# A router's chain reordered: last normalized rows, code numbers and gates behind the choice's signal, first expert's rows ahead of the block numbers

## The reference

```
g_logits = xt @ w_group + b_group                 # 4 per token; xt: RMS-normalized rows
g_p, g_idx = top_k(softmax(g_logits), 1)
e_logits = (xt @ w_expert + b_expert)[.., 4, 8]   # the 8 of the chosen group
e_top, e_idx = top_k(e_logits[g_idx], 2)
gate = g_p * softmax(e_top)                       # two gates per token
for each expert e, over the tokens that chose it, in blocks:
    y = (silu(x @ w_gate[e]) * (x @ w_up[e])) @ w_down[e]
out[token] += gate * y
```

## Time and profile before

| | us |
|---|---|
| median of three runs | 1797.62 |
| profiled execution | 1796.66 |
| its span, first to last instruction | 1795.0 |
| TensorE matmuls busy | 1679.6 (94%) |
| VectorE busy | 654.4 (36%) |
| ScalarE busy | 381.2 (21%) |
| GpSimd busy | 219.4 (12%) |
| share of TensorE in the chain that ended last | 78% |
| share of DMAs in it | 9% |

### The profile page before, as it was taken

How to read it: one execution, slowest core, us unless ns; L and a number is a source line. 1 busy time by engine, 2 the same in 40 slices (tenths; PEclk the granted TensorE clock), 3 DMA queues, 4 the chain that set the end, 5 groups by cost and what they waited for, 6 DMA issues and landing times.

```text
span 1795.0 us, 27891 instructions
## 1 busy us (share of the span) xinstructions
PE 1679.6 (94%) x9786; PEld 828.0 (46%) x9787; DVE 654.4 (36%) x1597; ACT 381.2 (21%) x878; POOL 219.4 (12%) x313
## 2 busy tenths in 40 slices
PE   7899889989899999999997999999999999999984
PEld 5466665545444444444432444555434343444331
DVE  2334488832322222222211656764222222222113
ACT  2233355521111111111110234341111111111012
POOL 1232024400000101010101200000001010101000
PEclk9899999999899999999999999999899999999988
DMA  6153149784489999999997700226599999999974
GB/s 186 50 157 112 27 152 304 253 316 179 158 350 416 420 415 422 412 422 412 420 412 296 279 1 1 77 114 245 205 422 414 421 419 418 411 419 409 418 329 155
DMA packets 84883, 513.81 MB, mean 286 GB/s; under 512 B 20821, under 2 KB 43302, under 8 KB 58586
## 3 DMA queue, kind: packets, MB, share of 16 engines
q1 hardware_dynamic: 66378, 463.45, 64.0%
q0 software_dynamic: 18416, 49.16, 8.3%
HBM read 499.65 MB, written 26.52 MB: 293 GB/s over the span
## 4 chain that ended last, share of the span: by engine, by line
PE 78%; DMA 9%; DVE 6%; issue 2%; ACT 2%; DVEq 1%; SPq 1%; ACTq 1%; POOLq 0%
PE ps L2083 70%; PE ps L2088 8%; DMA mem<-in_moe_w_down 4%; DMA mem<-in_moe_w_up 2%; DMA mem<-in_cache_mla 2%; DVE mem L1366 1%; ACT mem L801 1%; SPq L482 1%; DVE mem L1861 0%; ACTq L978 0%; DMA mem<-in_mla_w_a 0%; DMA mem<-moe_rows_back 0%; DVE mem L1832 0%; DMA mem<-in_mla_wq_b 0%; DVE mem L1824 0%
## 5 line engine op out<-in xcount | busy, mean ns | idle before, releaser
L2083 PE MATMUL ps<-mem 128*64 128x512 f32 (+14 forms) x8402 | 1515.7, 478 | 70.5 <-DMA mem<-in_moe_w_down 15.1
L2083 PEld LDWEIGHTS ps<-mem 128*64 128x64 f32 (+5 forms) x8402 | 665.0, 147 | 834.9 <-issue 755.1
L801 ACT ACTIVATE mem<-ps 128x512 f32<-128x512 f32 (+7 forms) x358 | 193.5, 546 | 574.7 <-PE ps L2083 402.5
L2088 PE MATMUL ps<-mem 64*128 64x64 f32 (+3 forms) x1384 | 202.2, 281 | 37.4 <-ACTq L978 7.0
L2088 PEld LDWEIGHTS ps<-mem 64*128 64x128 f32 (+3 forms) x1384 | 168.1, 182 | 123.4 <-issue 96.0
L1700 DVE TENSOR_TENSOR mem<-mem,ps 64x512 f32<-64x512 f32 x64 | 44.1, 690 | 414.6 <-ACT mem L1044 414.5
L736 POOL DMA_INDIRECT moe_rows_back<-mem x64 | 57.3, 896 | 840.5 <-DVE mem L1718 818.9
L1044 ACT ACTIVATE mem<-ps 64x512 f32<-64x512 f32 x64 | 37.7, 589 | 535.5 <-PE ps L2083 535.5
L1718 DVE COPY mem<-ps 64x512 f32<-64x512 f32 x64 | 44.4, 693 | 162.0 <-PE ps L2083 162.0
L1366 DVE STREAM_TRANSPOSE mem<-mem 128x2560 f32<-128x2560 f32 x32 | 89.2, 2824 | 15.7 <-DMA mem<-in_cache_mla 15.5
L686 POOL DMA_DIRECT2D mem<-in_cache_mla x96 | 51.7, 538 | 75.2 <-PE ps L2083 68.1
(11 more groups left out here) (240 smaller groups left out, 517.5 us busy)
## 6 DMA issues: line engine op xcount, KB each, us to landing
mem<-in_moe_w_gate SPq DMA_DIRECT2D x64, 2048.0 KB
mem<-in_moe_w_up SPq DMA_DIRECT2D x64, 2048.0 KB
mem<-in_moe_w_down SPq DMA_DIRECT2D x64, 2048.0 KB
mem<-in_cache_mla POOLq DMA_DIRECT2D x160, 160.0 KB, 3.7
mem<-in_cache_mla SPq DMA_DIRECT2D x96, 160.0 KB, 4.5
mem<-moe_rows_back SPq DMA_DIRECT2D x8, 1024.0 KB, 9.0
mem<-in_mla_wkv_b SPq DMA_DIRECT2D x8, 512.0 KB, 5.7
mem<-in_mla_wo SPq DMA_DIRECT2D x1, 4096.0 KB, 14.2
```

Source lines behind the costliest of these rows:

```text
L801: return act.activation(out, in_, ACT.Copy)
L2083: return pe.matmul(out, lhsT, rhs, start=start, stop=stop)
L2088: return pe.transpose(out, in_, ident[at:at + n, at:at + n])
```

## The change

On ScalarE the last tile is squared before its transposed copy, and the root comes after it (`root_of`). On VectorE the last `normed` leaves its place ahead of the last `logits`; `experts` calls it after the marks of block 1. The signal `sel_ready` follows the masked marks at once; the difference for the second gate and the code numbers come after it, and two memsets go. The gates move from ahead of `rank_mm` to behind the last `normed`. Then come the copy of the first rows and, one at a time between the steps of block 0, the row numbers of blocks 0 and 1, the marks of block 2 with the operand of block 2's rows, and the count of blocks. TensorE makes the first rows ahead of both `numbers`, and issues eight warming matmuls instead of nine. All of it holds for both layers.

```diff
 
                 square(L, T)
                 act.drain()
+                root_of(L, T)
+
+            def root_of(L, T):
+
                 act.activation(rstd[:, T:T + 1], sumsq[:, T:T + 1], ACT.Sqrt, bias=eps[:, 0:1], scale=1.0 / D
                                ).then_inc(sig["root_ready"], 1)
 
...
                     square_and_root(L, 2)
                     turned(L, 1)
                     square_and_root(L, PT)
-                for n_ in range(2, TILES):
+                for n_ in range(2, PT):
                     turned(L, n_)
-                square_and_root(L, PT - 1)
+                square(L, PT - 1)
+                turned(L, PT)
+                act.drain()
+                root_of(L, PT - 1)
 
                 act.wait_ge(sig["gsub_ready"], happened("gsub_ready", L + 1))
                 act.activation(tg[1], tg[0], ACT.Exp).then_inc(sig["gexp_ready"], 1)
...
             logits(0, 3)
             turned(0, 4)
             inverse(0, PT - 1)
-            normed(0, PT - 1)
             logits(0, 4)
             v.drain()
 
...
                 v.scalar_tensor_tensor(out=te[0], in0=te[1], scalar=-3e30, in1=te[0], op0=ALU.mult, op1=ALU.add)
                 v.drain()
                 first_largest(te[0], NE, t5[6], t5[1], te[3], te[2])
+                v.tensor_tensor(te[3], te[1], te[2], ALU.add)
+                v.drain()
+                v.tensor_tensor(te[4], te[3], over_last(valid, NE), ALU.mult)
+                v.drain().then_inc(sig["sel_ready"], 1)
+
                 v.tensor_tensor(t5[4], t5[6], t5[3], ALU.subtract).then_inc(sig["esub_ready"], 1)
-
-                v.tensor_tensor(te[3], te[1], te[2], ALU.add)
-                v.memset(rankm, -1.0)
-                v.memset(code, 0.0)
-                v.drain()
-                v.tensor_tensor(te[4], te[3], over_last(valid, NE), ALU.mult)
                 v.tensor_copy(code[:, 0, :, 0:NE], over_last(tokcode[:, 0], NE))
                 v.tensor_tensor(code[:, 1, :, 0:NE], te[2], over_last(tokcode[:, 1], NE), ALU.add)
-                v.drain().then_inc(sig["sel_ready"], 1)
-
-                v.wait_ge(sig["gexp_ready"], happened("gexp_ready", L + 1))
-                v.tensor_reduce(t5[2], tg[1], X, ALU.add)
-                v.wait_ge(sig["eexp_ready"], happened("eexp_ready", L + 1))
-                v.tensor_scalar(t5[7], t5[5], 1.0, None, ALU.add)
-                v.drain()
-                v.tensor_tensor(t5[6], t5[2], t5[7], ALU.mult)
-                v.drain()
-                v.reciprocal(gate1, t5[6])
-                v.drain()
-                v.tensor_tensor(gate2, gate1, t5[5], ALU.mult)
-
                 v.wait_ge(sig["rank_mm"], happened("rank_mm", L + 1))
                 v.scalar_tensor_tensor(out=te[3], in0=ps[:, 3, 0:TILES * NE].rearrange("p (t e) -> p t e", t=TILES),
                                        scalar=1.0, in1=te[4], op0=ALU.add, op1=ALU.mult)
...
                     v.tensor_scalar(fetch_at[b][0:BLK, :], ps[0:BLK, 4, 2 * b:2 * b + 1], FAR, None, ALU.add
                                     ).then_inc(sig["idx_ready"], 1)
 
-                for q in range(LOOK):
-                    if q >= 2:
-                        v.wait_ge(sig["idx_mm"], happened("idx_mm", FETCHES * L + q - 1))
-                    mark(q, q % 2)
-                    if q == 0:
-                        v.drain()
-                        v.tensor_tensor(direct, onehot[0], rstd[:, 0:TILES].unsqueeze(2).broadcast_to([P, TILES, BLK]), ALU.mult
-                                        ).then_inc(sig["direct_ready"], 1)
-                    else:
-                        if q == 2:
-                            v.drain()
-                            v.tensor_tensor(marks, onehot[0], rstd[:, 0:TILES].unsqueeze(2).broadcast_to([P, TILES, BLK]), ALU.mult
-                                            ).then_inc(sig["direct_ready"], 1)
-                        numbers(q - 1, (q - 1) % 2)
+                mark(0, 0)
+                v.drain()
+                v.tensor_tensor(direct, onehot[0], rstd[:, 0:TILES].unsqueeze(2).broadcast_to([P, TILES, BLK]), ALU.mult
+                                ).then_inc(sig["direct_ready"], 1)
+                mark(1, 1)
+                normed(L, PT - 1)
+                v.wait_ge(sig["gexp_ready"], happened("gexp_ready", L + 1))
+                v.tensor_reduce(t5[2], tg[1], X, ALU.add)
+                v.wait_ge(sig["eexp_ready"], happened("eexp_ready", L + 1))
+                v.tensor_scalar(t5[7], t5[5], 1.0, None, ALU.add)
+                v.drain()
+                v.tensor_tensor(t5[6], t5[2], t5[7], ALU.mult)
+                v.drain()
+                v.reciprocal(gate1, t5[6])
+                v.drain()
+                v.tensor_tensor(gate2, gate1, t5[5], ALU.mult)
 
                 v.wait_ge(sig["first_mm"], happened("first_mm", MADE * L + 1))
                 v.tensor_copy(sg[BLK:2 * BLK, :], ps[BLK:2 * BLK, 5, :]).then_inc(sig["first_dve"], 1)
-
-                v.tensor_scalar(lt[0:NE, 16:16 + MORE], blkat[0:NE, :], lt[0:NE, 0:1], None, ALU.is_lt)
-                v.drain()
-                v.reduce_sum(lt[0:NE, 1:2], lt[0:NE, 16:16 + MORE], X)
-                v.drain().then_inc(sig["nb_ready"], 1)
-
+                numbers(0, 0)
                 v.wait_ge(sig["xt_mm"], happened("xt_mm", NE * L + 1))
                 for c in range(2):
                     last = v.tensor_tensor(xeT[0][:, 4 * c:4 * c + 4], ps[:, 5 + 2 * c, 0:4 * BLK].rearrange("p (k t) -> p k t", k=4),
                                            gainT_ffn[:, L, 4 * c:4 * c + 4].unsqueeze(2).broadcast_to([P, 4, BLK]), ALU.mult)
                 last.then_inc(sig["xeT_ready"], 1)
+                numbers(1, 1)
+                mark(2, 0)
+                v.drain()
+                v.tensor_tensor(marks, onehot[0], rstd[:, 0:TILES].unsqueeze(2).broadcast_to([P, TILES, BLK]), ALU.mult
+                                ).then_inc(sig["direct_ready"], 1)
+                v.tensor_scalar(lt[0:NE, 16:16 + MORE], blkat[0:NE, :], lt[0:NE, 0:1], None, ALU.is_lt)
+                v.drain()
+                v.reduce_sum(lt[0:NE, 1:2], lt[0:NE, 16:16 + MORE], X)
+                v.drain().then_inc(sig["nb_ready"], 1)
 
                 v.wait_ge(sig["pre_mm"], happened("pre_mm", L + 1))
                 v.tensor_copy(lt[0:NE, 2:3], ps[0:NE, 3, 8:9])
...
             logits(1, 3)
             turned(1, 4)
             inverse(1, PT - 1)
-            normed(1, PT - 1)
             logits(1, 4)
             v.drain()
             experts(1)
...
                 start_more(pe, L, "idx_mm xt_mm gu_mm ht_mm d_mm")
                 pe.sem_inc(sig["more_d_mm"], 1)
                 pe.wait_ge(sig["lg_ready"], happened("lg_ready", TILES * L + PT))
-                keep_busy(9)
+                keep_busy(8)
                 pe.wait_ge(sig["sel_ready"], happened("sel_ready", L + 1))
                 sel, direct = te_both[L][4], directs[L]
                 mm(ps[:, 3, 0:TILES * NE], before, sel, True, False)
...
                         last = flip(ps[:, 5, k * BLK:(k + 1) * BLK], xe[b][0:BLK, k:D:KD])
                     last.then_inc(sig["xt_mm"], 1)
 
-                numbers(0, 0)
-                numbers(1, 1)
                 pe.wait_ge(sig["direct_ready"], happened("direct_ready", MADE * L + 1))
                 for T in range(TILES):
                     for c in range(2):
...
                         last = mm(ps[c * BLK:(c + 1) * BLK, 5, :].rearrange("p (f k) -> p f k", k=4), direct[:, T, :], rows,
                                   T == 0, T == TILES - 1)
                 last.then_inc(sig["first_mm"], 1)
+                numbers(0, 0)
                 pe.wait_ge(sig["first_act"], happened("first_act", MADE * L + 1))
                 pe.wait_ge(sig["first_dve"], happened("first_dve", MADE * L + 1))
                 for k in range(KD):
                     last = flip(ps[:, 5 + k // 4 * 2, k % 4 * BLK:(k % 4 + 1) * BLK], sg[k // 4 * BLK:(k // 4 + 1) * BLK, k % 4:FF:4])
                 last.then_inc(sig["xt_mm"], 1)
+                numbers(1, 1)
 
                 def place(i, r):
 
```

More of the change, by code:

```diff
@@ L1591, in experts @@
                 first_largest(te[0], NE, t5[6], t5[1], te[3], te[2])
-                v.tensor_tensor(t5[4], t5[6], t5[3], ALU.subtract).then_inc(sig["esub_ready"], 1)
                 v.tensor_tensor(te[3], te[1], te[2], ALU.add)
-                v.memset(rankm, -1.0)
-                v.memset(code, 0.0)
                 v.drain()
                 v.tensor_tensor(te[4], te[3], over_last(valid, NE), ALU.mult)
+                v.drain().then_inc(sig["sel_ready"], 1)
+                v.tensor_tensor(t5[4], t5[6], t5[3], ALU.subtract).then_inc(sig["esub_ready"], 1)
                 v.tensor_copy(code[:, 0, :, 0:NE], over_last(tokcode[:, 0], NE))
                 v.tensor_tensor(code[:, 1, :, 0:NE], te[2], over_last(tokcode[:, 1], NE), ALU.add)
-                v.drain().then_inc(sig["sel_ready"], 1)
```

(10 more changed lines are left out.)

## The result

Twenty runs of each kernel, taken beside each other: median 1792.66 us after (1787.16 to 1799.02), 1802.51 us before (1795.1 to 1808.2). The ratio is 0.9944, 95% interval 0.9931 to 0.9956, that is 10.1 us less, 7.9 to 12.4. The forecast was 9.0 us less. It named 1788.5 us, counted from a median of three runs (1797.62); twenty runs of the kernel before have a median of 1802.51, so the time after lies at 1792.66 although the gain was near the forecast.

What follows compares the result with a forecast made beforehand. The weight stream, started by TensorE's progress, was taken to bound the kernel. First rows ending 5.1 and 4.6 us earlier, less 0.2 and 0.5, gave 9.0 us, hence 1788.5 us; own range 1786 to 1792, whole range 1783 to 1796.

Steps and rivals of the forecast that it cites:

- What bounds it: Expert loops: the weight stream decides; if TensorE reaches the second expert earlier, the layer ends earlier, one for one.
- Step 1: Last tile's logits: scale and bias start directly behind TensorE's logits, not behind the normalized rows; gain 0.85 us a layer.
- Step 2: Router's choice: its signal follows the masked marks, without memsets and code operations ahead; gain 1.05 us a layer.
- Step 3: Layer 1's rank matmuls, 2.51 us against 1.87 in layer 0, gain from a shorter hole ahead: 0.3 us.
- Step 4: First rows ahead of both number groups on TensorE: they start 2.05 us earlier behind their operand.
- Step 5: Duration of the first rows, dependent on the clock: 6.3 us, range 4.3 to 8.6, against 7.45 and 6.7 before.
- clock stays up: Rival: full clock, first rows in 4.3 us in both layers, 4.0 us more gain, 1784.5 us; chance 0.17.
- Step 6: Work moved behind the first rows: 0.1 us a layer charged, 0.25 more for the clock, no wait for the gather.
- Own pace: Rival: the weights keep their own pace, so an earlier TensorE waits longer at expert 30; 1797.6 us, chance 0.07.
- late gather: Rival: block 1's gather lands after TensorE asks, 8.5 to 14.5 us lost; say 1800 us, chance 0.05.
- clock low in all first rows: Rival: low clock throughout, first rows in 8.6 us in both layers, 4.6 us less gain, 1793 us; chance 0.11.
- first condition: Row store ahead of block 1's gather, layer 0: issued at 473.2, takes its former 10.8 us and lands at 484.0.

Runs made afterwards that it cites:

- The two delays: Changed kernel with ten more warming matmuls (8.5 us) ahead of the first rows, in layer 0 or layer 1 only: ratios 0.9995 and 1.0002 to the kernel before.
- held-up gather: Changed kernel with eight more clearings of the gather's buffer on GpSimd in both layers: ratio 1.0052, 9.4 us above the kernel before.
- that half alone: Kernel before with only the first rows put ahead of both number groups: ratio 0.9976, 4.3 us under the kernel before.
- the eight above: Traced layers: four of the changed kernel, two with normalized rows back in front, one undelayed from each delay kernel; expert 4's issue at mean 48.2 us.

## Why the prediction was right, step by step

- **What bounds it: right.** The stream of weights starts with TensorE's progress and the layer's end follows one for one, within some 3.5 us. The two delays and the held-up gather show it.
- **Step 1, the last tile's logits: size right (0.85 forecast, 0.89 measured), cause incomplete.** The forecast named the root as no limit and the normalized rows as what goes, and the trace of before bears that out. It overlooked that the square ahead of the copy, which it mentions in passing, serves the same wait: with it, the rows in front cost nothing. As far as the trace of before tells, either would have earned the term, so the sum was not harmed.
- **Step 2, the choice's signal: right,** 1.05 forecast; steps 1 and 2 together 1.9 forecast, and 1.95 by the marks' end. But in layer 0 the ranks start later than the signal. The loads of the warming matmuls after the change show it:

```profile
462.46 0.34 PEld L2080 LDWEIGHTS ps<-mem 128*128 128x128 f32 x1 [0.52 <-issue]
...
468.99 0.19 PEld L2080 LDWEIGHTS ps<-mem 128*128 128x128 f32 x1 [0.24 <-issue]
469.42 0.19 PEld L2080 LDWEIGHTS ps<-mem 128*128 128x128 f32 x1 [0.24 <-DVEq L1601]
```

  Eight of them would have ended at 468.3, but the clock was low for some (a load each 0.86 us instead of 0.43), so they ran 0.2 us past the signal (469.2) and the ranks were done at 14.10, against 13.58 in both delay kernels, where they weren't slowed. Before, an idle of 2 us hid that. The forecast held that they would not delay. In layer 1 the same slowing cost nothing (14.36 against 14.37).
- **Step 3, the ranks of layer 1: about right.** Ranks were done at 14.36 and 14.63 instead of 16.14 to 16.89.
- **Step 4, the order: right,** 2.05 forecast, and 2.2 a layer by that half alone.
- **Step 5, the unknown term: mis-sized, on the careful side.** Forecast 6.3 us; of ten layers with the same order and eight warming matmuls ahead of the first rows (the eight above and both of the held-up gather), six had 4.6, the others 6.05 to 7.45, mean 5.4 with the 0.06 to start. The "clock stays up" rival is the common case for a layer, and the forecast lies above the mean of both cases. It made 1 us a layer. The kernel with three warming matmuls shows that this clock hangs on the thin stretch ahead, but the length of that stretch is not the whole of it: from the last warming matmul to the first rows it was 3.9 to 4.0 us in the six layers with 4.6, and 4.0, 4.0, 4.6 and 5.4 us in the other four. The traces show a split that the forecast did not look for. In all six the granted clock had already fallen to 0.50 among the warming matmuls, 4.0 to 4.5 us behind the transposes, and risen again; so slowed, these lasted up to the signal, and the ranks followed without idle time. In the other four it fell at 3.5 us or not among them at all, and TensorE was idle for 0.27 to 1.70 us ahead of the ranks. With three warming matmuls the clock fell among them at 4.2 us in layer 1, and fell again ahead of the ranks even so. What decides it was not tested. The Trainium skill (TensorE: Matmul & The Clock Gate, Part 1: The HAM clock gate) says that the number of slow matmuls at a start differs from run to run; the traces agree: layer 1 of the same kernel had 4.62 in one execution and 6.31 in the other.
- **Step 6, what moves behind: nothing lost, as forecast.** TensorE's wait ahead of the transposes of block 0 is 0.37 and ahead of expert 0 0.27, with the numbers in between. From the copy of the first rows to expert 0's matmuls it takes 2.49 us, against 2.48 before, so the 0.1 a layer charged was not needed. Nor was the 0.5 us set aside for the clock inside expert 0: its group takes 12.20 as before in the changed kernel. That it can come is shown by one delay kernel (13.80).
- **Rivals.** Own pace and late gather did not come; clock low in all first rows neither. The whole gain of the "clock stays up" rival, 13.0 us, lies above the measured interval. The late gather's first condition failed: the row store landed 2.9 us behind its issue instead of 10.7. But the room was smaller than I had it: the gather went out 29.03 us behind the transposes, at the late end of the forecast's 26.1 to 29.1, and TensorE asked at 35.18, not 36.6, which leaves 2.4 us.
- **Sum.** 9.0 forecast, 10.1 measured (7.9 to 12.4), 10.9 by the traces. Against the one trace of before that the forecast was counted from, the eight layers after give 12.2: 2.0 more by step 5, 0.7 that step 6 had taken off, and a little by the ranks. But that trace was long in this stretch (54.0 and 54.6, where six layers have a mean of 53.6), which takes 1.3 off again. So errors of opposite sign met, and part of the nearness is luck; the error of the times, 2 us either way, hides the rest.

## What to carry to other kernels

A transfer stream that is full for hundreds of microseconds turns its starting time into the end, so a serial stretch of small operations ahead of it is worth its whole length; find what issues the first transfer of the unbroken part and count back from there. When two edits serve the same wait, undo each of them alone, and both: here undoing the one that the change was named after lost nothing, which shows that it isn't needed beside the other, and not that the other is. How long TensorE has only thin work ahead of a dense group can be worth as much as the operations removed; splitting a thin stretch with dense work that has to be done anyway gave 1.7 us a layer here at no cost. Where that depends on how the clock happens to fall, one execution shows one case: trace several before sizing the term.

## What the runs showed of the hardware

- GpSimd's drain behind its clearing of a buffer took 9.6 to 10.2 us in layer 0 in every trace (9.6 with the row store long done, 10.2 with it just issued), and 1.8 to 7.5 us in layer 1. It stayed at 10.2 with eight more clearings behind it. What it waits for wasn't settled.
- The indirect gather of block 1's 64 rows in layer 0 landed in 3.4 to 3.8 us where it went out ahead of expert 3's weights (thirteen traces), and in 7.1 us where it went out behind them; in layer 1 in 3.0 to 6.2 us, and in 8.8 us with the gather held up.
- The store of 128 normalized rows by GpSimd in layer 0 landed 2.9 us behind its issue where it went out late, with the DMA engines idle, and 10.6 to 11.1 us behind it where it went out beside expert 2's gate and up weights.
- The granted clock fell to 0.50 and rose again among the warming matmuls in 20 of 28 layers traced, although TensorE ran them one behind the other, and each load then took 0.86 us instead of 0.43.
- What stands before the router (up to the last tile's transposes of layer 0) took 454.6 to 467.0 us over fourteen executions. That spread is larger than the change, and a single pair of the timed runs could have shown anything from -21 to +4 us.
